# All elimination steps of the triangular inverse moved behind the mLSTM loop on VectorE

## What is computed

```
m_low = where(strict, einsum(kb, k) * decay, 0)
sol = triangular_solve(m_low + eye(c), [v * beta | kb * exp(G)])      # needs (m_low + I)^-1
o, S = scan(step, s0, ...)                                            # 16 chunks, one after another
```

```
s = einsum(qc, kc) * exp(dc - mt)
num = w_inter * (qc @ cs) + s @ vc ;  den = w_inter * (qc @ ns) + sum(s)
cs = a_end * cs + (kc * wk)^T @ vc ;  ns = a_end * ns + kc^T wk
```

## Time and profile before

| | |
|---|---|
| median of three runs | 2635.62 us (2635.26 to 2638.98) |
| the profiled execution | 2634.22 us |
| its span, first to last instruction | 2632.6 us |
| mean granted TensorE clock, as a share of 2.4 GHz | 0.847 |
| TensorE busy | 2036.5 us (77%) |
| VectorE busy | 1031.5 us (39%) |
| ScalarE busy | 488.8 us (19%) |
| GpSimd busy | 530.9 us (20%) |

### The profile page before, as it was taken

The page is one execution under the profiler, slowest core; times in us unless marked ns, Lnnn a source line. Parts: engine busy times, 40 slices in busy tenths (PEclk is TensorE's granted clock), DMA queues, the critical chain, the costliest instruction groups (busy, mean ns, idle before and its releaser), DMA issues.

```text
span 2632.6 us, 28198 instructions
## 1 busy us (share of the span) xinstructions
PE 2036.5 (77%) x9888; PEld 1684.9 (64%) x9888; DVE 1031.5 (39%) x1987; ACT 488.8 (19%) x1073; POOL 530.9 (20%) x507
## 2 busy tenths in 40 slices
PE   5877786786534339599869885587899999999996
PEld 3544454454334338588846554464899999999995
DVE  4656665566458957323221401115311111111135
ACT  2211011111312123111120112102320310311311
POOL 0011110111134326110000000000433333433431
PEclk9988888888767669566679996678999999999998
DMA  3000000000042222111151000021111111111111
GB/s 109 32 20 28 18 28 18 18 22 20 10 89 59 39 33 56 62 37 54 36 209 53 32 16 0 26 75 43 34 47 44 44 48 40 48 40 48 48 40 66
DMA packets 65912, 117.75 MB, mean 45 GB/s; under 512 B 18055, under 2 KB 46743, under 8 KB 65143
## 3 DMA queue, kind: packets, MB, share of 16 engines
q1 hardware_dynamic: 62374, 105.21, 13.0%
q0 software_dynamic: 3472, 11.73, 1.4%
HBM read 102.94 MB, written 13.98 MB: 44 GB/s over the span
## 4 chain that ended last, share of the span: by engine, by line
PE 42%; DVE 4%; ACT 2%; DMA 1%; issue 1%; ACTq 0%; DVEq 0%
PE ps L2179 9%; PE ps L2180 9%; PE ps L2181 9%; PE ps L2086 8%; DVE regH L2365 1%; PE ps L2125 1%; PE ps L2112 1%; DVE rows L2363 1%; PE ps L2161 1%; PE ps L2052 1%; PE ps L2119 1%; PE ps L2059 1%; ACT feat L2272 1%; DMA feat<-ck_in 0%; DMA feat<-cv_in 0%
## 5 line engine op out<-in xcount | busy, mean ns | idle before, releaser
L2179 PE MATMUL ps<-feat_r,rows_r 128*128 128x352 f32 x1536 | 501.7, 327 | 31.7 <-DVE regH_r L2370 20.2
L291 PE MATMUL ps<-regH,regW 128*128 128x352 f32 x1296 | 419.5, 483 | 7.3 <-DVE regH L510 7.3
L2181 PE MATMUL ps<-feat_r,regW_r 128*128 128x352 f32 x1152 | 373.9, 325 | 0.0
L291 PEld LDWEIGHTS ps<-regH,regW 128*128 128x128 f32 x1296 | 263.4, 204 | 162.7 <-issue 32.6
L2179 PEld LDWEIGHTS ps<-feat_r,rows_r 128*128 128x128 f32 x1536 | 292.6, 190 | 34.2 <-issue 29.8
L2347 DVE TENSOR_TENSOR regA<-ps,regA 128x352 f32<-128x352 f32 (+1 forms) x144 | 75.5, 524 | 473.7 <-PE ps L2181 304.5
L2180 PE MATMUL ps<-feat_r,rows_r 128*128 128x352 f32 x768 | 249.6, 325 | 0.0
L2180 PE MATMUL ps<-regH_r,rows_r 128*128 128x352 f32 x768 | 248.4, 323 | 0.0
L2181 PEld LDWEIGHTS ps<-feat_r,regW_r 128*128 128x128 f32 x1152 | 220.2, 191 | 0.0
L2036 POOL TENSOR_TENSOR rows_r<-regW,cst 128x1024 fp32r<-128x1024 f32 x48 | 94.5, 1969 | 430.6 <-PE ps L2181 333.9
L2431 DVE TENSOR_TENSOR feat_r<-feat,feat_r x96 | 51.8, 539 | 317.5 <-ACT feat_r L2252 317.5
(11 more groups left out here) (444 smaller groups left out, 3157.7 us busy)
## 6 DMA issues: line engine op xcount, KB each, us to landing
regW<-w_ff_in SPq DMA_DIRECT2D x48, 512.0 KB, 3.5
regW<-w_in_in SPq DMA_DIRECT2D x27, 512.0 KB, 3.4
ext<-w_ff_in SPq DMA_DIRECT2D x16, 512.0 KB, 3.4
regA<-xT_in SPq DMA_DIRECT2D x3, 1408.0 KB, 10.6
regA<-xT_in SPq DMA_DIRECT2D x1, 4224.0 KB, 22.1
yT_out<-regH SPq DMA_DIRECT2D x3, 1408.0 KB, 5.5
feat<-ck_in POOLq DMA_DIRECT2D x8, 512.0 KB, 3.9
feat<-cv_in POOLq DMA_DIRECT2D x8, 512.0 KB, 3.9
```

The costliest lines, as they stand in the source:

```text
L291: ins = pe.matmul(ps[b][:, 0:BW], ring[slot][:, k * P:(k + 1) * P], hv[:, k, blk(b)], start=(k == 0), stop=(k == KT - 1))
L2179: pe.matmul(ps[b][:, 0:BW], hi, rhs_hi(k, b), start=(k == 0), stop=False)
L2181: ins = pe.matmul(ps[b][:, 0:BW], lo, rhs_hi(k, b), start=False, stop=(k == KT - 1))
```

## The change

The portions leave the loop, and the wait for `v_in` and all 62 steps stand behind it. The steps, their operands and their order among themselves are the same, as is `slots`, which nothing uses now. No other engine's list changes.

```diff
                 for c in range(UN):
                     if c + 1 < UN:
                         ml_keys(c + 1)
-                    if c == 1:
-                        dve.wait_ge(sem("v_in"), 16)
-                    eliminate_until((2 * c - 1) / slots)
                     ml_state(c)
                     if c + 1 < UN:
                         ml_scores(c + 1)
                     ml_squares(c)
-                    if c >= 1:
-                        eliminate_until(2 * c / slots)
+                dve.wait_ge(sem("v_in"), 16)
                 eliminate_until(1.0)
                 dve.memset(V[:, 0:4096:65], 1.0).then_inc(sem("inv"), 1)
```

## The result

The changed kernel takes 2673.09 us (median of four, 2670.30 to 2686.03), where the kernel before took 2635.44 us beside it (median of four). The ratio is 1.0152, with an interval of 1.0117 to 1.0187: slower, by some 40 us (31 to 49). The forecast was 2670.5 us.

A forecast was written before the change was run, and what follows sets the result against it. VectorE was taken to bound the stage from 806.5 to 953.95 us, elimination covering the mLSTM's waits. Loop 70.9 + elimination 111.4 - 147.45 = +34.85 us on 2635.6 gave 2670.5 us; 8-in-10 range 2661 to 2682.

The forecast's parts named there:

- elimination, alone: VectorE's 124 elimination operations behind the mLSTM loop: 106.1 us, plus 4.2 of steps between them and 1.1 of remaining collision.
- loop, from 806.5 on: mLSTM loop after `V` arrives, without elimination: ends at 877.4 us, so lasts 70.9 us, of which VectorE works 22.
- rounds of two chunks: State of chunk c to state of c + 2, in series: request, row transfer 9.46, GpSimd 4.06, TensorE 8.2, state 1.41; 23.2 us.
- tail behind the state of chunk 6: Chunk 7's scores' product 0.98, `ml_back` 3.5, state 1.41 and squares 0.55 us, ending the loop at 877.4 us.
- the rival by which the change does not reach the end: Output of `V` waits for something other than the memset, so the change is hidden: 2635.6 us, chance 0.01.
- The collision: In the stage before, GpSimd's SBUF reads block VectorE's two-input elimination operations; 16.3 us disappear once elimination stands alone.
- The 1.1 us kept for `dn_prepare(2)`: Collision left beneath the moved elimination, from GpSimd's last delta-rule preparation: 1.1 us, bounds 0 and 2.7.
- between that and 9.74 I take 8.2: TensorE's front and back in each round: 7.2 us with slow front and fast back, 9.74 at half clock; 8.2 taken.
- the second rival: Row transfers of chunks 4 and 6 slowed 4 us each by overlapping requests: +8 us more, 2678.6 us, chance 0.12.
- TensorE stays fast: Clock does not fall between the loop's bursts, each 4.95 us: +24.8 us, 2660.4 us, chance 0.08.
- Neutral: Rounds shorter than their sum, with the loop at 36.05 us from 806.5 on, so no change in time; chance 0.02.
- faster: Collision decides: VectorE finds mLSTM inputs ready, loop 22 us, waits under 14 us; -14.05 us, 2621.6 us, chance 0.02.

The follow-up runs named there:

- the aligned version: Kernel before with larger portions, key copies on ScalarE, and GpSimd's mask sum and `qw` product started by signals from VectorE's mLSTM operations: 2617.89 us, ratio 0.9922.

## Why the prediction was right

The time came as forecast, and mostly by the terms that were to make it. That the whole lies within 2.6 us of the forecast is in part luck: the stage came out 2.2 us under its term (32.7 for 34.9), and in the profiled execution the parts outside it, which the prediction held still, added 3.4 us.

| step | forecast | measured |
|---|---|---|
| elimination, alone | 111.4 us | 877.71 to 989.55: 111.8 us |
| its 124 operations | 106 to 109 us | 107.5 us |
| loop, from 806.5 on (+2.58 us for the later start) | 70.9 us | 809.08 to 877.71: 68.6 us |
| VectorE's waits in the loop | 49 us | 47.2 us |
| rounds of two chunks | 23.2 us | 23.9 and 22.5 us |
| tail behind the state of chunk 6 | 6.44 us | 871.67 to 877.71: 6.0 us |
| way of the inverse and beginning of the delta rule | unchanged | 16.79 us before (953.95 to 970.75), 16.48 after |
| sum of the stage | +34.9 us | +32.7 us |

**What carries the end of the stage.** Right. The memset moved from 953.95 to 989.56, and what stands behind it kept its distance: SyncE's request follows by 0.14 us in both. So the rival by which the change does not reach the end is out. The forecast of 989 us was met by the later start; from the request of chunk 2's rows the memset came 185.5 us on, where the sum had 187.3.

**The collision.** Right in size and cause: 122.4 - 107.5 = 14.9 us. The cut of GpSimd's work takes 14.5 us from the elimination of the kernel before and 0.3 from that of the kernel after, and the aligned version has the relief without the move. The 1.1 us kept for `dn_prepare(2)` came out as about 1.4, spread over the first small steps; the product on 180 elements took 0.69 us where 0.155 us + 180 x 1.043 ns = 0.34.

**The round.** Right in its mechanism; the run without row transfers shows it by taking the transfer away (11.1 us for two chunks), though TensorE's fast clock comes with that. One term was mis-sized: "between that and 9.74 I take 8.2" for TensorE. The front and back took 823.87 - 817.55 = 6.3, 6.3 and 7.6 us, under the lower bound of 7.2 in two of three. TensorE's timeline of the first of them shows why:

```profile
817.55 2.93 PE L1056 MATMUL ps<-feat,regH 128*128 128x128 f32 x12 [7.35 <-POOL regH L977]
820.27 0.59 PE L1062 MATMUL ps<-cst,feat 128*128 128x128 f32 x3
820.69 0.49 PE L1065 MATMUL ps<-cst,feat 128*128 128x128 f32 x3
...
822.98 0.89 PE L1087 MATMUL ps<-regH,regW 128*128 128x130 f32 x6
```

The twelve products ran at the slow rate (2.93 us), but the rest of the burst was already at the fast one: L1065's three transposes, at 820.69, took 0.49 and not 0.85 us, L1087's six products 0.89 and not 1.43. I had taken a slow front to be slow to its end, 4.2 us. The prediction also calls the back fast in four of the five bursts before; in one of these four the last six products (L1087 at 862.86) took 1.57 us.

**The transfers.** From request to GpSimd's start the six took 9.43, 8.97, 12.04, 10.32, 9.35 and 9.60 us. The 10.32 of chunk 5 are no transfer's: GpSimd was busy with chunk 4's work until then. Only chunk 4's was longer, 837.38 - 825.34 = 12.04 us, above the highest (10.29) that the bounds allowed. Chunk 5's rows were requested at 831.14, while it was under way, and that looks like the second rival: one place of its two, 2.6 us and not 4. But other traces speak against its cause. Chunk 6's transfer had the same company (854.76, 5.5 us behind) and took 9.35 us, and in the kernel without elimination chunk 4's had it too (821.31, the next request at 826.84) and took 9.86. In the kernel with half portions chunk 4's transfer took 11.21 us, and the next request came when it was over:

```profile
829.05 0.37 SPq L879 DMA_DIRECT2D regW<-row_scratch  x1
841.26 0.37 SPq L879 DMA_DIRECT2D regW<-row_scratch  x1
```
```profile
840.26 1.80 POOL L981 TENSOR_TENSOR regW<-regW,acc 128x768 f32<-128x768 f32 x1 [12.32 <-DMA regW<-row_scratch]
```

So some transfers are 2 to 3 us longer, with another request under way and without. The 2.6 us and TensorE's shorter bursts, 1.9, 1.9 and 0.6 us under the 8.2, partly cancel in the rounds, and the sum fits better than its parts: that is luck too.

**The rivals.** *TensorE stays fast*: each burst behind a long gap (7.35, 11.78 and 9.35 us) began at the slow rate, though two of three, at 6.3 us, lie nearer to this rival's 4.95 than to 9.74. *Neutral* and *faster* needed a loop of 36.05 us and waits under 14 us; the trace has 68.6 and 47.2. The run without row transfers is what the neutral case looks like: rounds of 11.1 us and a ratio of 1.0017.

**Slips in the working that moved nothing.** The neutral case's rounds of "some 9 to 10 us" don't follow from its 36.05 us: from the end of chunk 0's state at 801.41 to the state of chunk 6, with the tail of 6.44 behind it, three rounds have 34.7 us, 11.6 each. The first rival's terms add up to +24.6 us, not +24.8. "TensorE at half clock in both" has its row for the 17 us only: in the chunk loop the clock was 0.75 from 971 to 980 us and 1.00 from 980 to 1000. And the wait for GpSimd's end and the operation's own time give 1.62 + 0.56 = 2.18 us where 2.05 was measured; GpSimd's mask sum was longer there as well, 2.08 us in place of 1.80.

**What stays open.** Why chunk 4's transfer was longer here, and one in the kernel with half portions. How much of the round's fall without transfers belongs to TensorE's clock: that was not tried by itself. And the 2.6 us ahead of the stage, which other kernels show in both directions.

## What to carry to other kernels

Work in portions between the operations of a dependent chain is covered as long as the portions last as long as the chain's waits; moving it out costs the waits, not its own length, so find the longest round trip of the chain (here one transfer of rows) and make the portions at least as long as that: here half of them was nearly enough, and a quarter was not. Before giving such an overlap up for a collision, look whether the colliding engine's work can be let go beside operations that it doesn't disturb: this kept both, 20 us under the kernel before. And look at what stands behind the last portion: the output of the interleaved work had a way of 17 us, and with the end of the chain beneath it the stage was 6.7 us shorter.

## What the runs showed of the hardware

**TensorE regained its clock within a burst, but not after the same time.** Each burst of the loop that came after 7.35 to 11.8 us of idleness began slow. Of the three, the one shown above ran L1065 at the fast rate (0.49 us) at 820.69, 3.1 us after its start, and so did the second; the one that began at 862.64 still ran L1065 in 0.85 us, the slow figure, 3.4 us in. In the kernel before, one burst after 8.32 us of idleness was slow for 9.7 us, its back included. In the run without row transfers, where TensorE had next to no gaps in the loop, the front was never slow.

**Not all of GpSimd's work costs VectorE the same.** Mask sums, `qw` products and key copies of six chunks together cost VectorE's elimination 14.5 us; the copies, 27% of that work by their time, only 1.2. Beside VectorE's state and squares, which take one operand from PSUM or have a single input, GpSimd's mask sum kept its 1.80 us and theirs stayed 1.38 and 0.55. The Trainium skill ("SBUF — State Buffer", section "Who interferes with whom") says that a VectorE instruction with two SBUF inputs and a GpSimd instruction that reads SBUF exclude each other; the traces agree in which operations are hit. That the place of GpSimd's work counts and not its amount is what 105.9 against 115.1 us for the same work shows.

**A transfer is not always as long.** One set of rows took 12.04 us from request to use and another 11.21, where all others for which GpSimd stood ready took 8.8 to 10.9. The first had another set requested 5.8 us behind it, the second had none, and sets with such company also took 9.35 and 9.86 us: the company alone doesn't explain it.
